# Expert weights in one 2 MB transfer instead of two of 1 MB, from the sixth pass of each expert loop on

## The reference, cut to what matters

```
def swiglu(x, w_gu, w_dn):
    g, u = jnp.split(x @ w_gu, 2, axis=-1)
    return (jax.nn.silu(g) * u) @ w_dn
...
    def step(acc, inp):
        t, wb, ei = inp
        y = swiglu(x_pad[t], w_gu[ei], w_dn[ei])
        return acc.at[t].add(y.astype(jnp.float32) * wb[:, None]), None
```

## Time and profile before

| | |
|---|---|
| median of 3 runs (lowest, highest) | 1265.64 us (1265.19, 1266.31) |
| span of the profiled execution, first to last instruction | 1263.2 us |
| mean granted TensorE clock | 0.950 |
| TensorE busy | 1089.7 us, 86% |
| VectorE, ScalarE busy | 505.3 us (40%), 248.6 us (20%) |
| DMA, mean over the span | 398 GB/s |

### The profile page before, as it was taken

How to read it: one execution, slowest core, us unless ns; L and a number is a source line. 1 busy time by engine, 2 the same in 40 slices (tenths; PEclk the granted TensorE clock), 3 DMA queues, 4 the chain that set the end, 5 groups by cost and what they waited for, 6 DMA issues and landing times.

```text
span 1263.2 us, 17095 instructions
## 1 busy us (share of the span) xinstructions
PE 1089.7 (86%) x6524; PEld 597.4 (47%) x6524; DVE 505.3 (40%) x1131; ACT 248.6 (20%) x575; POOL 0.4 (0%) x5
## 2 busy tenths in 40 slices
PE   7999999997887878687869999999788797878785
PEld 6887586543333424243326678655333242434332
DVE  3697975334123122212226887533312222312231
ACT  1021722211001111111113472221101111101110
POOL 0000000000000000000000000000000000000000
PEclk9999999999889899999989999999988998989998
DMA  9999999999999999999999927899999999999996
GB/s 346 392 409 414 407 360 362 414 423 422 424 423 423 423 424 422 424 424 424 422 416 392 406 104 276 355 411 423 422 424 424 423 423 424 423 423 424 424 424 279
DMA packets 99289, 502.24 MB, mean 398 GB/s; under 512 B 10985, under 2 KB 35462, under 8 KB 44934
## 3 DMA queue, kind: packets, MB, share of 16 engines
q1 hardware_dynamic: 98742, 500.92, 97.1%
q10 hardware_dynamic: 464, 0.20, 0.1%
HBM read 500.04 MB, written 1.05 MB: 397 GB/s over the span
## 4 chain that ended last, share of the span: by engine, by line
SPq 49%; PE 31%; DMA 9%; DVE 5%; issue 4%; ACT 0%; DVEq 0%
SPq L595 44%; PE bank L779 25%; DMA ring<-in_moe_w_gate_up 4%; SPq L704 3%; PE bank L782 2%; DMA ring<-in_ada_w 2%; DMA w_gu_x<-in_ada_w 2%; DMA ring<-in_moe_w_down 1%; SPq L602 1%; PE bank L906 1%; PE bank L1055 1%; DVE s_sb L1809 1%; PE bank L1264 1%; PE bank L978 1%; DVE s_sb L1803 1%
## 5 line engine op out<-in xcount | busy, mean ns | idle before, releaser
L779 PE MATMUL bank<-w_gu,ring 128*32 128x512 f32 (+1 forms) x1120 | 294.9, 703 | 107.3 <-DMA w_gu<-in_moe_w_gate_up 34.1
L779 PEld LDWEIGHTS bank<-w_gu,ring 128*32 128x32 f32 (+1 forms) x1120 | 77.5, 133 | 273.5 <-issue 273.0
L1963 DVE TENSOR_TENSOR hh<-sg,bank 128x256 f32<-128x256 f32 x44 | 27.3, 621 | 399.2 <-ACT sg L1549 399.2
L779 PE MATMUL bank<-ring 128*32 128x512 f32 (+1 forms) x336 | 169.7, 654 | 10.2 <-DMA gate<-in_moe_w_gate_up 7.8
L779 PE MATMUL bank<-w_gu,hhT 128*32 128x512 f32 (+1 forms) x416 | 138.4, 596 | 7.3 <-DMA ring<-in_moe_w_down 4.9
L779 PE MATMUL bank<-w_dn,ring 128*32 128x512 f32 x240 | 130.1, 792 | 16.5 <-DMA w_dn<-in_moe_w_gate_up 8.2
L779 PE MATMUL bank<-w_gu_x,ring 128*32 128x512 f32 (+1 forms) x272 | 127.0, 669 | 5.5 <-DMA ring<-in_moe_w_gate_up 5.5
L1549 ACT ACTIVATE sg<-bank 128x256 f32<-128x256 f32 x44 | 16.9, 384 | 480.5 <-PE bank L779 480.5
L1980 DVE SCALAR_TENSOR_TENSOR bank<-bank,w_slot,gate 128x512 f32<-128x512 f32 x88 | 66.6, 759 | 97.3 <-PE bank L779 97.2
L779 PE MATMUL bank<-sel,h_hi 128*128 128x256 f32 x352 | 87.8, 290 | 0.0
L1429 ACT ACTIVATE y_hi<-bank 128x512 fp32r<-128x512 f32 x88 | 52.6, 597 | 162.0 <-DVE bank L1980 161.8
(11 more groups left out here) (317 smaller groups left out, 1706.4 us busy)
## 6 DMA issues: line engine op xcount, KB each, us to landing
w_gu<-in_moe_w_gate_up SPq DMA_DIRECT2D x130, 1024.0 KB, 25.5
w_gu<-in_moe_w_down SPq DMA_DIRECT2D x46, 1024.0 KB, 26.4
ring<-in_moe_w_gate_up SPq DMA_DIRECT2D x42, 1024.0 KB, 26.2
ring<-in_ada_w SPq DMA_DIRECT2D x36, 1024.0 KB, 11.6
w_gu_x<-in_moe_w_gate_up SPq DMA_DIRECT2D x30, 1024.0 KB, 26.0
w_dn<-in_moe_w_gate_up SPq DMA_DIRECT2D x28, 1024.0 KB, 26.3
w_gu_x<-in_moe_w_down SPq DMA_DIRECT2D x14, 1024.0 KB, 26.4
w_dn<-in_moe_w_down SPq DMA_DIRECT2D x14, 1024.0 KB, 26.0
```

Of the source, the lines that this page charges most:

```text
L779: return nc.tensor.matmul(o, a, b, start=first, stop=last)
L1963: v.tensor_tensor(hh[:, :].rearrange("s (f p) -> s p f", f=FE // P), sg[:, :].rearrange("s (p f) -> s p f", f=FE // P), bank[b][:, FE:2 * ...
```

## The change

Passes 0 to 4 load as before. From pass 5 on (49 of 64 experts in each loop) a gate-up matrix comes in one transfer of 2 MB, 128 runs of 16 KB, into two neighbouring places. Seven such pairs are formed: the four gate-up buffers, `w_gu_x`, `w_dn_0`, and `xn` with `hT`, which are now one tile `xn_hT`. A pair is loaded when both of its places have been read, and TensorE waits for the whole matrix before half 0. Down matrices take the place that is read first, on a tie one of the single places 14 to 17. The numbers of some places change (`hT` is now 13).

```
 def weight_items(p):
     js = positions(p)
+    if p >= WHOLE_FROM:
+        return [("gu", j, WHOLE) for j in js] + [("dn", j, 0) for j in js]
     return [("gu", j, half) for half in range(2) for j in js] + [("dn", j, 0) for j in js]
...
+            if item[0] == "gu" and item[2] == WHOLE:
+                u = min(range(0, 2 * PAIRS, 2), key=lambda u: (max(free[u], free[u + 1]), u))
+            elif p >= WHOLE_FROM:
+                u = min(free, key=lambda u: (free[u], u < 2 * PAIRS, u))
+            else:
+                u = min(free, key=lambda u: (free[u], u))
...
-        ADA_4_UNIT = (16, 17, 9, 7, 11, 5, 6, 8)
+        ADA_4_UNIT = (13, 17, 9, 7, 11, 5, 6, 8)
...
-                eng.wait_ge(sem(f"gu_done{l}"), 2 * PASS_OF[j] + 1 + half)
+                eng.wait_ge(sem(f"gu_done{l}"), 2 * PASS_OF[j] + 1 + min(half, 1))
...
+                elif kind == "gu" and half == WHOLE:
+                    dst, src = whole_at[u // 2].rearrange("p (k n) -> p k n", k=KT), gu_src[l](e)
...
-                            wait_unit(pe, l, ("gu", j, half))
+                            if half == 0 or gu_item(j, half)[2] != WHOLE:
+                                wait_unit(pe, l, gu_item(j, half))
```

More of the change, by code:

```diff
@@ L114 @@
 UNITS = 19
-ROWS_UNIT, RING_UNIT = 18, 13
-ROUTER_UNIT = 17
+ROWS_UNIT, RING_UNIT = 18, 16
+ROUTER_UNIT, HT_UNIT, SECOND_UNIT = 17, 13, 15
+PAIRS = 7
 SHARED = ("dn", "shared", 0)
@@ L132, in reading_order, with units_of @@
     return turns
+def units_of(item, unit):
+    u = unit[item]
+    return (u, u + 1) if item[0] == "gu" and item[2] == WHOLE else (u,)
 def assign_units():
@@ L142, in turn_read @@
             return turn_of["shared_down"]
-        return turn_of[("gu", PASS_OF[j], half) if kind == "gu" else ("dn", PASS_OF[j])]
+        return turn_of[("gu", PASS_OF[j], min(half, 1)) if kind == "gu" else ("dn", PASS_OF[j])]
     unit = dict(EARLY_UNITS + LATE_UNITS + LAST_UNITS)
     users = {u: [item] for item, u in unit.items()}
-    free = [(turn_read(item), u) for item, u in unit.items() if u != ROWS_UNIT] + [(turn_of["shared_up"], 15), (turn_of["shared_up"], 16),
-                                                                                   (-1, ROUTER_UNIT), (-1, RING_UNIT)]
+    signals = {u: [item] for item, u in unit.items()}
+    free = {u: turn_read(item) for item, u in unit.items() if u != ROWS_UNIT}
+    free.update({SECOND_UNIT: turn_of["shared_up"], HT_UNIT: turn_of["shared_up"], ROUTER_UNIT: -1, RING_UNIT: -1})
     loads = []
@@ L152, in assign_units @@
         for item in loads[-1]:
-            i = min(range(len(free)), key=lambda i: free[i])
-            _, u = free.pop(i)
-            unit[item] = u
[L156 to L161, removed]
+            if item[0] == "gu" and item[2] == WHOLE:
[4 more added lines that the diff above has]
+                u = min(free, key=lambda u: (free[u], u))
+            unit[item] = u
+            for v in units_of(item, unit):
+                users.setdefault(v, []).append(item)
+                free[v] = turn_read(item)
+            signals.setdefault(u, []).append(item)
+    return unit, users, signals, loads
+UNIT, USERS, SIGNALS, LOADS = assign_units()
 CO, _at = {}, 0
@@ L230, in build @@
         x = sb("x", [P, NT, D])
-        xn = sb("xn", [P, NT, D])
-        hT = sb("hT", [P, KT, N])
+        xn_hT = sb("xn_hT", [P, 2, CH])
+        xn = xn_hT[:, 0, :].rearrange("p (t d) -> p t d", t=NT)
+        hT = xn_hT[:, 1, :].rearrange("p (k n) -> p k n", k=KT)
         gate_all = sb("gate", [P, 3, D])
@@ L457, in ring_of @@
             return (i + 4) % RING
+        whole_at = [w.rearrange("p k n -> p (k n)") for w in w_gu_0 + w_gu_1]
+        whole_at += [w_gu_x[:, :, :].rearrange("p h n -> p (h n)"), w_dn_both[:, :, :, :].rearrange("p u f d -> p (u f d)"),
+                     xn_hT[:, :, :].rearrange("p h n -> p (h n)")]
         unit_at, xg = [], []
@@ L465, in build @@
             unit_at.append(halves + [w_gu_x[:, h, :] for h in range(2)] + [w.rearrange("p f n -> p (f n)") for w in w_dn_0]
-                           + [xn[:, :, :].rearrange("p t n -> p (t n)"), ring[:, free[0], :], ring[:, a, :], ring[:, b, :],
-                              hT[:, :, :].rearrange("p k n -> p (k n)"),
+                           + [xn_hT[:, 0, :], xn_hT[:, 1, :], ring[:, a, :], ring[:, b, :], ring[:, free[0], :],
                               gate_all[:, 0:2, :].rearrange("p a d -> p (a d)"), w_gu_y[:, :]])
@@ L471, in build @@
                 xg_rings = free[1:]
-                unit_of_ring = {free[0]: 13, a: 14, b: 15}
-        ADA_4_UNIT = (16, 17, 9, 7, 11, 5, 6, 8)
+                unit_of_ring = {free[0]: RING_UNIT, a: 14, b: SECOND_UNIT}
+        ADA_4_UNIT = (13, 17, 9, 7, 11, 5, 6, 8)
         ADA_4_PE, ADA_4_ACC = 3, 4
@@ L480, in wait_between, with gu_item @@
         def wait_between(eng, u):
-            eng.wait_ge(sem(f"unit_in{u}"), 16 * (len(USERS[u]) + 1))
+            eng.wait_ge(sem(f"unit_in{u}"), 16 * (len(SIGNALS[u]) + 1))
+        def gu_item(j, half):
+            return ("gu", j, half) if ("gu", j, half) in UNIT else ("gu", j, WHOLE)
         def gu_half(l, j, half):
-            return unit_at[l][UNIT[("gu", j, half)]].rearrange("p (k n) -> p k n", k=KT // 2)
+            item = gu_item(j, half)
+            return unit_at[l][UNIT[item] + (half if item[2] == WHOLE else 0)].rearrange("p (k n) -> p k n", k=KT // 2)
         def down_of(l, item):
@@ L577, in unit_load @@
                 u = UNIT[item]
[L578 to L588, removed]
+                for v in units_of(item, UNIT):
+                    before = USERS[v].index(item) - 1
+                    if before >= 0:
+                        wait_read(sp, l, USERS[v][before])
+                    elif v == 12:
+                        sp.wait_ge(sem("xT_ps"), 4 * (2 * l + 2))
+                    elif v == 14:
+                        freed(sp, ("sgu", l, 0))
+                    elif v in (SECOND_UNIT, HT_UNIT):
+                        freed(sp, ("sgu", l, 1))
+                    elif v == ROUTER_UNIT:
+                        sp.wait_ge(sem("logits"), l + 1)
                 if item == SHARED:
                     dst, src = down_of(l, item), by_rows(t["moe_shared_down"][l])
+                elif kind == "gu" and half == WHOLE:
+                    dst, src = whole_at[u // 2].rearrange("p (k n) -> p k n", k=KT), gu_src[l](e)
                 elif kind == "gu":
```

3 lines of the change are left out of this document (2 added, 1 removed).

## The result

The changed kernel takes 1275.03 us, the median of four runs (1274.24 to 1276.42). Against the kernel before the ratio is 1.0078, with a 95% interval of 1.0064 to 1.0092: 9.9 us slower (9.4 by the two medians). One of the four runs of the kernel before that stand beside it took 6024.46 us and is not in the ratio. The profiled execution took 1274.92 us, with a span of 1273.0 us, 9.8 more than before.

The account below looks back on a forecast made before the run. The prediction took weight transfers as the bound in the expert loops. On a span of 1263.2 us, -7.0 + 12.0 + 3.5 = +8.5 us gave 1271.7, and 2.4 us more gave 1274.1 us; range 1267 to 1282.

Parts of the forecast that it names:

- The bound and the gain: In both expert loops, transfers are the bound without gaps; 16 KB runs save 3.5 us per loop, -7.0 us in all.
- The line through the rates of shorter runs: Time per run in the DMA queue: 0.0366 ns per byte plus 9.0 ns per run, giving 609 ns for 16 KB.
- the rival that the engines split the run: In the loops' gate-up loads, engines split each 16 KB run in two: no gain, prices unchanged, 1281 us; chance 10%.
- The last pass: In pass 21 of each loop, half 0 cannot start before the last gate-up landing (T): +6.0 us per loop, +12.0 together.
- The soft term: Length of half 0 in pass 21: 6.35 us taken, bounds 3.6 us at full clock and 7.2 us at 1.2 GHz.
- Behind loop 0: Layer 1's first loads wait for pass 21's down product; the third lands 11.7 us behind f = 1's start: +3.5 us.
- the upper bound of 3.5 + 3.2: Behind loop 0, 3.2 us more than the +3.5 us if TensorE's clock falls during the waits for loads.
- What costs nothing (places): Mid-loop, waiting for both places of a pair costs nothing; the tightest case, in pass 7, has a margin of 2.4 us.
- The sum: Whole kernel: -7.0 + 12.0 + 3.5 = +8.5 us on the span, plus 2.4 us to the median: 1274.1 us.

Follow-up runs that it names:

- e4_two_8k: The changed kernel, same places and waits, but each gate-up matrix moved in two 1 MB transfers with 8 KB runs: 1281.41 us, ratio 1.0127 to the kernel before.
- e2_last_halves: The changed kernel with the four gate-up matrices of each loop's last pass loaded as two halves again: 1266.17 us, ratio 1.0010 to the kernel before.
- e1_places: The changed kernel with other places, so no last-pass matrix lies where the first in_ada_w loads behind loop 0 go: 1269.45 us, ratio 1.0030 to the kernel before.
- e9_fill3: The changed kernel with 3 unused matmuls on TensorE before each of the first three in_ada_w waits behind loop 0: 1272.78 us, ratio 1.0060 to the kernel before.
- e8_fill20: The changed kernel with 20 unused matmuls on TensorE just before half 0 of the last pass: 1274.57 us, ratio 1.0078 to the kernel before.
- e3_both: The changed kernel with the last pass in halves and its matrices kept off the places in_ada_w loads need: 1260.61 us, ratio 0.9958 to the kernel before.

## Why the prediction was right, step by step

- **The bound and the gain (-7.0 us).** Right, the size a little too large. The loops' rate went to 427 GB/s (428 forecast). The gain alone is 6.2 us by the ratios of e4_two_8k and the changed kernel, and 2.7 + 3.5 = 6.2 us by the distance from the first load to T in the kernels before and after. That these agree to a tenth is chance: the second trace of the changed kernel gives 5.2 us by the same distance. The line through the rates of shorter runs held for one more doubling, and the rival that the engines split the run falls, since 784 packets per engine are gone. The Trainium skill ("DMA: Bandwidth & Descriptors", section "Where 436 GB/s comes from") has a ceiling of 435.2 GB/s; the 427 of these stretches lie below it.
- **The last pass (+6.0 us per loop).** The mechanism was right, the size a little too large. In the profile f = 1 starts at T + 14.7 in loop 0 (16.1 forecast; before T + 10.1), so +4.6 us (in the second trace of the changed kernel at T + 16.0, +5.8), and in loop 1 at T + 15.8 (1247.20 to 1263.00; before T + 10.0), so +5.8. The soft term was the one named: half 0 took 5.2 us (641.88 to 647.06) at a granted clock of 0.68 in loop 0 and 6.3 us at 0.55 in loop 1, where 6.35 had been put in. Putting the halves back (e2_last_halves) gave 8.6 us for the two loops, with four matrices of each loop back at 8 KB runs.
- **Behind loop 0 (+3.5 us).** The mechanism was right and the size too small, 6.0 us by the trace, inside the upper bound of 3.5 + 3.2. The third group starts 12.7 us behind the start of f = 1 (656.57 to 669.30), where 11.7 was worked out: the second and third load did not follow at 2.47 us each, their groups start 2.8 and 3.1 us apart, with the pieces of `kv_w_down` issued 0.5 us behind the third. No run shows whether those pieces are the reason. That makes 4.5 us (8.2 before). The rest, 1.5 us, is the clock, which the prediction had as its bound: the last two groups took 1.88 us for 1.04. e1_places took all of it back, 6.1 us; in e9_fill3 `kv_w_down` follows the third group by 3.76 us, as before the change, for 5.26, so the part of the clock is gone there.
- **What costs nothing (places).** Right within what the profile can tell. The rate between 300 and 640 us has no hole, and 8 KB runs in the same places (e4_two_8k) reach 423 GB/s for 424 before. Loop 1's T came 0.4 us sooner than before in that kernel, loop 0's 1.6 later.
- **The sum.** 1274.1 us was forecast and 1275.0 measured, +8.5 and +9.9 us. Of the 2.4 us that the forecast adds to the span, some 0.5 is the distance of that execution from the median: in each run listed the time is 1.8 to 2.0 us above its own span. The prices came to 15.5 us in the sum and to 16.1 us in e4_two_8k. That they agree so well owes something to chance: by the experiments about 2.8 us less went into the last pass (8.6 us, and 0.6 us for the eight matrices that lost their longer runs there, against 12.0) and 2.6 more into the stage behind loop 0 (6.1 against 3.5).

## What to carry to other kernels

In this kernel longer runs gained about what a line of time per run against bytes said (6.2 us, 7.0 forecast), but a transfer twice as large is also a signal that comes half as often: look at the last consumer of the stream, where nothing hides the wait for the whole, and keep the small pieces there. When a planner picks places anew, follow what each place's next user outside the loop then waits for; here one wait behind the loop, which another choice of places avoids, cost as much as the longer runs gained. An idle wait can cost twice on TensorE, first the wait and then a low clock behind it: here that second price was about 4.4 of 9.9 us.

## What was not expected of the hardware

The same idle time did not always have the same clock behind it. In e8_fill20 TensorE idled 2.13 us ahead of T in loop 0 and 2.15 in loop 1, after 8.90 us of matmuls in both; its timeline there:

```profile
632.08 8.90 PE L808 MATMUL bank<-cst 128*128 128x256 f32 x40
643.11 0.63 PE L808 MATMUL bank<-w_gu,ring 128*32 128x512 f32 x3 [2.13 <-DMA w_dn<-in_moe_w_gate_up]
...
1236.97 8.90 PE L808 MATMUL bank<-cst 128*128 128x256 f32 x40
1248.02 0.63 PE L808 MATMUL bank<-w_gu,ring 128*32 128x512 f32 x3 [2.15 <-DMA w_dn<-in_moe_w_gate_up]
1248.45 0.80 PE L808 MATMUL bank<-w_gu,ring 128*32 128x512 f32 x3
1248.96 1.14 PE L808 MATMUL bank<-w_gu,ring 128*32 128x512 f32 x3
```

The table by stretch has the granted clock behind each:

```profile
643.10:646.60 3.50, 3.49 (x32) 1.11 (x32) 0.00 (x0) 0.00 (x0) 0.00 (x0) 1.00 1.03 410
...
1248.00:1251.00 3.00, 2.98 (x20) 1.15 (x24) 0.00 (x0) 0.00 (x0) 0.00 (x0) 0.63 1.02 408
```

In loop 0 the clock stayed at 1.00 (2.4 GHz). In loop 1 the matmuls went from 0.63 to 1.14 us, and the clock of the stretch was 0.63, so most of it was at 1.2 GHz. What made the difference is not shown. Behind loop 0 it is alike: in e2_last_halves the second and third group took 1.04 us each after waits of 1.85 and 1.83 us, and in the changed kernel 1.89 and 1.88 us after waits of 1.74 and 1.18.

And T in loop 0 scatters more between kernels with the same order and size of transfers than the rate explains, from 458.7 to 460.1 us behind the first load in those with 16 KB runs in all passes from the sixth on, against 456.6 to 457.3 in loop 1. In e3_both, whose last pass is in halves, it is 460.7. The cause stays open.
